# Rotary half-swap taken from DMA transfers to ScalarE copies out of PSUM, with the sink as a column of the scores

## The reference, cut to what matters

```python
def rope(x, pos):
    ...
    x1, x2 = xf[..., : A_HD // 2], xf[..., A_HD // 2:]
    return jnp.concatenate([x1 * cos - x2 * sin, x2 * cos + x1 * sin], axis=-1).astype(x.dtype)

def sink_softmax(s, sinks):
    sk = sinks[:, :, None, None]
    m = jnp.maximum(jnp.max(s, axis=-1, keepdims=True), sk)
    p = jnp.exp(s - m)
    return p / (jnp.sum(p, axis=-1, keepdims=True) + jnp.exp(sk - m))
```

## Time and profile before

| what | value |
|---|---|
| median of 3 runs | 1087.24 us (1086.41 to 1088.52) |
| the profiled execution, its own time | 1086.28 us |
| its span | 1084.4 us |
| PE busy | 1067.0 us, 98% of the span |
| DVE, ACT, POOL busy | 688.1, 520.3, 125.5 us |
| the stage of the change | about 775.2 to 846.2 us of the span |

### The profile page before, as it was taken

How to read it: one execution, slowest core, us unless ns; L and a number is a source line. 1 busy time by engine, 2 the same in 40 slices (tenths; PEclk the granted TensorE clock), 3 DMA queues, 4 the chain that set the end, 5 groups by cost and what they waited for, 6 DMA issues and landing times.

```text
span 1084.4 us, 21272 instructions
## 1 busy us (share of the span) xinstructions
PE 1067.0 (98%) x8066; PEld 1050.4 (97%) x8066; DVE 688.1 (63%) x1053; ACT 520.3 (48%) x812; POOL 125.5 (12%) x158
## 2 busy tenths in 40 slices
PE   8999999999999999999999999999999999999997
PEld 7999999999999999999999999999977999999997
DVE  7766665466557766665547666655698776666541
ACT  6544443356675544443335444433466554444332
POOL 5000001100005300000110000011232600000011
PEclk9999999999999999999999999999999999999999
DMA  6554454335433644455434444544443344445531
GB/s 233 196 183 163 155 214 161 134 114 190 141 127 123 215 166 182 155 184 181 177 117 163 182 159 158 209 158 158 142 150 104 117 156 169 179 155 187 183 134 44
DMA packets 26354, 173.90 MB, mean 160 GB/s; under 512 B 3876, under 2 KB 5320, under 8 KB 7752
## 3 DMA queue, kind: packets, MB, share of 16 engines
q1 hardware_dynamic: 24288, 168.93, 44.0%
q0 software_dynamic: 1248, 2.92, 0.8%
q10 hardware_dynamic: 776, 1.48, 0.4%
HBM read 169.28 MB, written 2.57 MB: 158 GB/s over the span
## 4 chain that ended last, share of the span: by engine, by line
PE 92%; DVE 3%; DMA 1%; issue 1%; POOL 1%; ACT 1%; SPq 0%; DVEq 0%; ACTq 0%
PE acc L441 30%; PE acc L442 29%; PE acc L443 29%; DVE wlo L428 1%; DMA x<-in_xT 1%; DMA raw<-in_w 0%; POOL work L1505 0%; DVE work L1295 0%; DVE work L1311 0%; DVE xs L1081 0%; POOL work L1501 0%; PE mb L627 0%; PE mb L462 0%; PE num L636 0%; PE num L610 0%
## 5 line engine op out<-in xcount | busy, mean ns | idle before, releaser
L441 PE MATMUL acc<-xs,whi 128*128 128x288 f32 x1696 | 503.5, 297 | 2.6 <-DVE xs L1081 1.8
L442 PE MATMUL acc<-xs,whi 128*128 128x288 f32 x1696 | 498.6, 294 | 0.0
L443 PE MATMUL acc<-xs,wlo 128*128 128x288 f32 x1696 | 498.6, 294 | 0.0
L404 ACT ACTIVATE whi<-raw 128x1024 fp32r<-128x1024 f32 (+1 forms) x290 | 326.3, 1126 | 356.9 <-PE acc L443 334.1
L428 DVE TENSOR_TENSOR wlo<-raw,whi 128x1024 fp32r<-128x1024 f32 (+1 forms) x290 | 386.3, 1332 | 160.8 <-ACT whi L404 150.4
L441 PEld LDWEIGHTS acc<-xs,whi 128*128 128x128 f32 x1696 | 318.2, 188 | 6.5 <-DVE xs L1081 2.2
L442 PEld LDWEIGHTS acc<-xs,whi 128*128 128x128 f32 x1696 | 318.3, 188 | 0.4
L443 PEld LDWEIGHTS acc<-xs,wlo 128*128 128x128 f32 x1696 | 318.2, 188 | 0.0
L441 PE MATMUL acc<-fs,whi 128*128 128x288 f32 x832 | 245.6, 295 | 0.9 <-DVE fs L1323 0.7
L442 PE MATMUL acc<-fs,whi 128*128 128x288 f32 x832 | 244.6, 294 | 0.0
L443 PE MATMUL acc<-fs,wlo 128*128 128x288 f32 x832 | 244.6, 294 | 0.0
(11 more groups left out here) (224 smaller groups left out, 589.0 us busy)
## 6 DMA issues: line engine op xcount, KB each, us to landing
raw<-in_w SPq DMA_DIRECT2D x113, 1024.0 KB, 4.8
raw<-in_w SPq DMA_DIRECT2D x32, 1408.0 KB, 6.0
work<-work SPq DMA_DIRECT2D x40, 36.0 KB, 1.9
x<-in_xT SPq DMA_DIRECT2D x4, 288.0 KB, 6.4
raw<-in_w SPq DMA_DIRECT2D x4, 256.0 KB, 5.3
work<-row_bounce ACTq DMA_DIRECT2D x1, 640.0 KB, 5.5
work<-in_cst POOLq DMA_DIRECT2D x1, 560.0 KB, 4.1
work<-in_c POOLq DMA_DIRECT2D x1, 514.0 KB, 4.4
```

The costliest lines, as they stand in the source:

```text
L404: act.activation(dst, src, ACT.Copy).then_inc(hi_done, 1)
L441: pe.matmul(out, wh, hi[:, k, :], start=(first and n == 0), stop=False)
L442: pe.matmul(out, wh, lo[:, k, :], start=False, stop=False)
L443: mm = pe.matmul(out, wl, hi[:, k, :], start=False, stop=(last and n == len(tiles) - 1))
```

## The change

The half-swap is made by ACT: four copies of 32 rows each straight out of the PSUM bank into `s_swap` (`half_swap`). DVE multiplies the bank by the cosine (`turned_by_cos`) where it copied it before. Both the sine product and the sum are POOL's (`turned`). No transfer is left. ACT's copies wait for DVE's product (`t1_ready`), and a bank is free when ACT's copies are done (`raw_ready`); the counter `evac` counts only the v groups in this stage. In ACT's program the copies of piece n stand ahead of the weight split of piece n + 4, from n = 2 on. At the start of the stage both cosine products of k0 and q0 stand behind the norm, since they need `rc`. The transposes of v0 move behind q2. The negated sink is written by POOL into a column of `prob` next to the scores (`sink_column`), so that one exponential with its sum takes the sink in; the exponential of the sink (L1000) and the addition (L1307) are gone.

```diff
-TURN_AFTER = {"q1": "v0", "v1": "v1"}
+TURN_AFTER = {"q2": "v0", "v1": "v1"}
...
-                        for at in range(0, P, HD // 2):
-                            of = at ^ (HD // 2)
-                            sp.dma_start(s_swap[at:at + HD // 2, xi % 2, :], s_raw[of:of + HD // 2, xi % 2, :])\
-                                .then_inc(swap_in[xi % 2], 16)
...
-                    for j, (lo_, hi_) in enumerate(parts):
-                        v = prob[:, t % 4, lo_:hi_]
-                        act.activation(v, v, ACT.Exp, scale=-1.0, bias=s_neg[:, b, j:j + 1], accum_out=s_sum[:, b, j:j + 1])
-                    act.activation(s_sk[:, b, 0:len(parts)], s_neg[:, b, 0:len(parts)], ACT.Exp, bias=sink).then_inc(exp_ready, 1)
+                    act.wait_ge(sink_ready, t + 1)
+                    for j, (lo_, hi_) in enumerate(parts_of(t)):
+                        v = prob[:, t % 4, lo_:hi_ + 1] if j == 0 else prob[:, t % 4, lo_ - 1:hi_]
+                        ins = act.activation(v, v, ACT.Exp, scale=-1.0, bias=s_neg[:, b, j:j + 1], accum_out=s_sum[:, b, j:j + 1])
+                    ins.then_inc(exp_ready, 1)
...
+                def half_swap(p):
+
+                    xi = ROPE.index(p)
+                    act.wait_ge(t1_ready, xi + 1)
+                    if xi >= 2:
+                        act.wait_ge(t2_ready, xi - 1)
+                    for at in range(0, P, HD // 2):
+                        of = at ^ (HD // 2)
+                        ins = act.activation(s_swap[at:at + HD // 2, xi % 2, :],
+                                             group_bank(group_of("piece", p))[of:of + HD // 2, :], ACT.Copy)
+                    ins.then_inc(raw_ready, 1)
+
                 for what, p in SWA_EVENTS:
                     if what == "piece":
-                        hi_ahead(0, c0_ + SWA_PIECES.index(p))
+                        n = SWA_PIECES.index(p)
+                        if n < 2:
+                            hi_ahead(0, c0_ + n)
+                        if p in ROPE:
+                            half_swap(p)
+                        if n >= 2:
+                            hi_ahead(0, c0_ + n)
...
-                    own(dve.tensor_tensor(s_den[:, b, 0:J], s_sum[:, b, 0:J], s_sk[:, b, 0:J], ALU.add))
-                    own(dve.reciprocal(s_inv[:, b, 0:J], s_den[:, b, 0:J]))
+                    own(dve.reciprocal(s_inv[:, b, 0:J], s_sum[:, b, 0:J]))
...
+            def turned_by_cos(c0_, n, xi, bank):
+
+                dve.wait_ge(piece_done, c0_ + n + 1)
+                if xi >= 2:
+                    dve.wait_ge(rope_done, xi - 1)
+                dve.tensor_tensor(s_t1[:, xi % 2, :], bank, rc, ALU.mult).then_inc(t1_ready, 1)
+
...
-                            dve.tensor_copy(s_raw[:, xi % 2, :], bank).then_inc(evac, 1)
+                        elif n >= 2:
+                            turned_by_cos(c0_, n, xi, bank)
...
-                            dve.tensor_tensor(rc, cos, rstd[:, :], ALU.mult).then_inc(rcs_ready, 1)
                             dve.tensor_scalar(neg_snk, snk, -1.0, None, ALU.mult)
                             dve.tensor_scalar(neg_snks, snks, -1.0, None, ALU.mult)
-                            own(dve.tensor_tensor(rs, sin, rstd[:, :], ALU.mult))
+                            own(dve.tensor_tensor(rc, cos, rstd[:, :], ALU.mult))
+                            dve.tensor_tensor(rs, sin, rstd[:, :], ALU.mult).then_inc(rcs_ready, 1)
+                            for xi in range(2):
+                                turned_by_cos(c0_, xi, xi, group_bank(xi))
...
-                        dve.tensor_tensor(s_t2[:, xi % 2, :], s_swap[:, xi % 2, :], rs, ALU.mult).then_inc(t2_ready, 1)
...
+                    if n >= 4:
+                        pool.wait_ge(pt_mm, n - 3)
...
+                    pool.tensor_copy(dst, sink_of(n, neg_snk, neg_snks).to_broadcast([P, n_col])).then_inc(sink_ready, 1)
...
-                pool.tensor_tensor(s_t1[:, b, :], s_raw[:, b, :], rc, ALU.mult).then_inc(t1_ready, 1)
+                pool.wait_ge(raw_ready, xi + 1)
+                pool.tensor_tensor(s_t2[:, b, :], s_swap[:, b, :], rs, ALU.mult).then_inc(t2_ready, 1)
```

123 lines of the change are left out of this document (71 added, 52 removed).

## The result

The changed kernel took 1102.82 us (median of 4 runs, 1101.69 to 1103.07) against 1087.26 us for the kernel before on the same chip (4 runs, 1086.41 to 1088.52). The ratio is 1.0137, with a 95% interval of 1.0125 to 1.0148: slower, by 15.6 us and not by the 7.35 of the forecast, and 3.8 us above the range. The profiled execution took 1101.69 us with a span of 1099.9 us.

What follows compares the result with a forecast made beforehand. It took the kernel to be bound by a chain through DVE and ACT, ACT's weight split waiting behind the copies. 5.0 + 3.8 - 1.45 = + 7.35 us gave 1094.6 us, range 1089.2 to 1099 for 8 in 10.

Steps and rivals of the forecast that it cites:

- The bound, and the chain: One round through DVE and ACT, with ACT's weight split behind four copies: 6.66 us against 5.99, 0.67 us more a round.
- crossing: Step from one engine to another that waits for it, taken as 0.03 us each.
- The price of the four copies: Four ACT copies of 32 rows by 288 from PSUM, each stepping 0.29 us, 1.16 us together.
- The upper bound: ACT's copies as if none overlapped the next: 0.38 us each, 1.52 us for four.
- Rival 2: It costs more: copies don't overlap (nine swaps, 0.36 more each) or PE's clock falls; 1095.5 to 1099.5 us, chance 0.16.
- v1's round: Round whose piece has no copies, ACT's split directly following its exponential: about 5.4 us, 0.6 less than before.
- The collisions of the start: Three DVE weight splits (pieces 5, 6, 7) run beside POOL's products before the first score: + 1.35 us.
- The end: At tick 16 PE no longer waits for POOL's rotated q7, only for the scores of tick 15: - 1.45 us.
- The clock: PE's long wait behind q3 may halve its clock; one 11.6 us round exceeds the loop by 5, 4 being slack.
- The start, 5.0: First score comes 5.0 us later: 3.65 from DVE and ACT taking turns, 1.35 from POOL's products beside DVE's splits.
- The seven rounds, 3.8: First score to tick 14: six rounds with a rotated piece at 0.67 us more, with smaller corrections, + 3.8 us.
- The sink column and the move of the transposes: POOL's sink columns and moving v0's transposes behind q2 were costed at nothing; the move saves an early PE wait.

## Why the prediction was right in kind and wrong in size

- **The bound, and the chain** (ACT's split behind the copies behind the product, DVE's split and the next scores behind ACT's): right, and shown by the run with the split first. Every crossing, and every term but one, came within 0.04 us. One link was half luck: in the rounds ACT is busy with its own exponentials until the product is there, which the prediction did not see; with that wait turned round three of the rounds stayed as they were.
- **The price of the four copies** is the step that failed: "so 0.29 for 288: 1.16". It took the step of copies that follow each other in the same rows, and for these it is right (0.30 us from the single copy to the split behind it). The four begin in other rows each time, and stepped 0.41 us, 1.65 for four; the copies cut by columns and the two of 64 rows show that it is this. Four sets in the start make 4 x 0.49 = 1.96 of the 1.94 us missing there, and six in the rounds 2.9 of the 4.65. Together that is 4.9 of the 7.6 us between forecast and profile. That the start comes out to 0.02 us is partly luck: the prediction's own walk gave k0's and q0's copies 1.1 and 1.0 us and not 1.16 each, 0.2 too little, and its collisions on the path were 0.3 too many. The upper bound, 0.38, also had no overlap and was too low, since it took the duration of 256 columns for that of 288 (0.402). Rival 2 then counted nine swaps on the chain, where its sum has four in the start and six in the rounds: with ten at the measured price the same sum gives 1094.6 + 4.9 = 1099.5, above the range. And the case had only part of a chance of 0.16, though the rows of before hold no two copies of ACT in different rows: nothing stood for 0.29 against 0.38.
- **The rule of the Trainium skill** that was set aside (ScalarE: Activation LUTs, What ACT_TABLE_LOAD costs) gives 0.43 us for a copy of 288 columns and an overlap of 93 ns, a step of 0.33. The duration, 0.40 here, lies a little under it. The step was nearer to 0.41 than the prediction's 0.29 and still too short: an overlap of about 0.1 us is there in the 72-column copies, 0.24 at a step of 0.12, and not in the 32-row ones.
- **v1's round**: forecast 0.6 us shorter, it was 0.19 longer. ACT's split does follow its exponential directly, but POOL's sum for q6 (835.89, 0.93 us) and its copy of the sample columns behind it fall on DVE's split (836.08), which takes 1.83 us instead of 1.22 (the row is below). The prediction priced such meetings in the start and left them out of the rounds. In the last round there is another (1.72), + 0.5.
- **The collisions of the start**: forecast 1.35, measured 1.55, of which 1.05 lie on the path. Right in kind; that piece 5's collision hides in DVE's wait for ACT was overlooked. What the Trainium skill says (SBUF — State Buffer, SBUF: two separate sides), DVE and GpSimd on one pair of ports, agrees: POOL's work made splits of 1.72 to 1.85 us out of 1.22, and the cosine product out of PSUM stayed at 0.44 beside it.
- **The end**: forecast -1.45, measured -0.44. PE did not wait for POOL at tick 16 any more, as foreseen. But it waited 2.80 us at L714, and the clock was down behind that; with the clock full the end was 0.79 us shorter (15.08), so 0.8 of the difference of 1.0 is this.
- **The clock**: it was named among what could go wrong, with the right place (behind q3). It did fall there, and cost nothing: with PE kept busy the clock stayed up and the seven rounds took the same 49.15 us. The rival was wrong in what such a fall costs while DVE and ACT hold the chain. The Trainium skill's warning (TensorE: Matmul & The Clock Gate, HAM oscillation — how this bites in real kernels) was that a wait of PE costs the full clock afterwards. The trace agrees with it for the falls behind 7.14 and 2.80 us, not for the wait of 2.81 us with the clock at 1.00; and of the two falls only the second cost time.
- **The start, 5.0**, would have been 6.96 with the measured copies, against 6.94. The seven rounds, 3.8, would have been 6.7 against 8.45: 1.1 of what is left are the two collisions, and 0.6 are spread over the rounds' crossings.
- **The sink column and the move of the transposes**, "at nothing": the first is worth 3 to 3.6 us, of which the chain's sum had a part (the shorter way to the inversion); the second seems to cost about 1 us in the kernel without the chain, at the edge of what the runs can tell.

The collisions in the sixth and in the seventh round, on DVE:

```profile
836.08 1.83 DVE L437 TENSOR_TENSOR wlo<-raw,whi 128x1024 fp32r<-128x1024 f32 x1
...
844.25 1.72 DVE L437 TENSOR_TENSOR wlo<-raw,whi 128x1024 fp32r<-128x1024 f32 x1 [2.13 <-ACT whi L413]
```

## What to carry to other kernels

Work that is moved to an engine with free time is paid in full if it stands, in that engine's program, ahead of what the fullest engine waits for: here the order of two calls was worth 14 us, and the work itself at most 1 us. So go round the loop engine by engine before the busy times are believed, and put first what others wait for. Where the trace has no two neighbours of the new kind (here, copies in different rows), give no overlap its full chance, and price what lengthens a neighbour's work when the two run side by side (here POOL's products and DVE's splits) in every round and not only at the start.

## What the runs showed of the chip

- An ACT copy out of PSUM that began in another row than the one before it did not overlap it: four of 32 x 288 span 1.65 us at 0.402 each, with a shift of rows or without, two of 64 x 288 span 0.82 at 0.405. Copies that began in the same row overlapped by about 0.1: 32 x 144 takes 0.274 and steps 0.18 to 0.19, 128 x 72 takes 0.24 and steps 0.12, and a split behind a copy of 128 x 288 (0.41) starts after 0.30. Starting rows 32 and 64 apart were tried; what in the engine holds them is not known from these runs.
- A copy of 128 rows (0.410 us) costs what one of 32 does (0.402).
- A split of DVE takes 1.22 us alone and 1.72 to 1.85 beside POOL's work.
- The granted clock went to 0.50 behind waits of PE of 7.14 and 2.80 us in the changed kernel, and of 2.76 and 2.23 in two others (split first; sink column with moved transposes). It stayed at 1.00 behind one of 2.81 us in the version with PE kept busy 45 us earlier. Behind the wait of 7.14 us the lower clock cost nothing, as another chain ruled; behind that of 2.80 it cost 0.8, and behind that of 2.23, where PE was the limit of the rounds behind it, PE took 1.2 us longer for the same products.
